# The head loop of a fused two-block transformer kernel: scores issued two heads ahead, and a projection tile moved in front of the loop

## The reference, cut to what matters

```
oa = moba_attention(qa, ka, heads(va, N_HEADS_A))
ob = dsa_attention(qb, kb, heads(vb, N_HEADS_B), qi, ki, wi)
oc = stick_breaking_attention(heads(qc, N_HEADS_C), ...)
...
log_1m = jnp.where(strict, jax.nn.log_sigmoid(-z), 0.0)
after = lax.cumsum(log_1m, axis=3, reverse=True) - log_1m
a = jnp.where(strict, jnp.exp(log_beta + after), 0.0)
...
o = (_rms(o).reshape(B, S, D_MIX) * out_g[layer]).astype(x.dtype)
x = x + g2 * (o @ w_out[layer])
```

## Time and profile before

| | |
|---|---|
| median of 3 runs | 2841.31 us (2838.57 to 2844.32) |
| the profiled execution | 2839.58 us |
| its span in the profile | 2837.5 us |
| granted TensorE clock, mean | 0.992 of 2.4 GHz |
| head loop, first layer | 2009.04 to 2060.49 us |
| head loop, second layer | 2564.74 to 2618.29 us |

### The profile page before, as it was taken

How to read it: one execution, slowest core, us unless ns; L and a number is a source line. 1 busy time by engine, 2 the same in 40 slices (tenths; PEclk the granted TensorE clock), 3 DMA queues, 4 the chain that set the end, 5 groups by cost and what they waited for, 6 DMA issues and landing times.

```text
span 2837.5 us, 37822 instructions
## 1 busy us (share of the span) xinstructions
PE 2766.8 (98%) x16120; PEld 2426.8 (86%) x16120; DVE 1951.3 (69%) x2187; ACT 1366.8 (48%) x1562; POOL 228.7 (8%) x201
## 2 busy tenths in 40 slices
PE   8999999999999999999999999999899999999999
PEld 6889999998888889999998887878878878788787
DVE  6668876655666678877655667677876676677644
ACT  5444545455444445545454444444644444446433
POOL 0000420000000000520000000003000000030000
PEclk9999999999999999999999999999999999998999
DMA  8655433445766655333446666653266676442454
GB/s 306 257 220 183 149 125 136 164 164 210 263 261 248 248 208 189 138 136 132 171 165 228 257 255 243 260 218 134 90 244 251 239 274 253 177 150 95 176 189 148
DMA packets 82038, 564.42 MB, mean 199 GB/s; under 512 B 9072, under 2 KB 10576, under 8 KB 15952
## 3 DMA queue, kind: packets, MB, share of 16 engines
q1 hardware_dynamic: 66272, 465.47, 44.8%
q0 software_dynamic: 15600, 96.55, 9.0%
HBM read 560.86 MB, written 1.12 MB: 198 GB/s over the span
## 4 chain that ended last, share of the span: by engine, by line
PE 78%; DVE 13%; ACT 4%; POOL 2%; issue 2%; DMA 1%; SPq 0%; POOLq 0%; ACTq 0%; DVEq 0%
PE ps L332 71%; DVE ring_lo L327 4%; ACT w_hi L320 2%; POOL qk L2038 1%; PE ps L899 1%; POOL rope_a L2034 1%; DVE a_hg L1806 1%; DMA rows<-mod_rows 1%; DMA ring<-stream 1%; DVE e L1786 1%; DVE e L1785 1%; PE ps L1287 1%; DVE h_lo L576 0%; PE ps L1416 0%; PE ps L1442 0%
## 5 line engine op out<-in xcount | busy, mean ns | idle before, releaser
L327 DVE TENSOR_TENSOR ring_lo<-ring,w_hi 128x2048 fp32r<-128x2048 f32 x422 | 973.8, 2310 | 484.0 <-ACT w_hi L320 473.0
L320 ACT ACTIVATE w_hi<-ring 128x2048 fp32r<-128x2048 f32 x422 | 806.4, 1911 | 318.6 <-PE ps L332 188.0
L332 PE MATMUL ps<-w_hi,h_hi 128*128 128x512 f32 (+1 forms) x1920 | 728.9, 380 | 18.1 <-DVE ring_lo L327 9.0
L332 PE MATMUL ps<-w_hi,h_lo 128*128 128x512 f32 (+1 forms) x1920 | 717.0, 373 | 0.0
L332 PE MATMUL ps<-ring_lo,h_hi 128*128 128x512 f32 (+1 forms) x1920 | 716.3, 373 | 0.0
L332 PEld LDWEIGHTS ps<-w_hi,h_hi 128*128 128x128 f32 x1920 | 363.7, 189 | 85.6 <-DVE ring_lo L327 11.3
L332 PE MATMUL ps<-h_hi,w_hi 128*128 128x256 f32 x1488 | 431.6, 290 | 1.4 <-DVE h_lo L576 1.3
L332 PE MATMUL ps<-h_lo,w_hi 128*128 128x256 f32 x1488 | 423.0, 284 | 0.0
L332 PE MATMUL ps<-h_hi,ring_lo 128*128 128x256 f32 x1488 | 423.0, 284 | 0.0
L332 PEld LDWEIGHTS ps<-w_hi,h_lo 128*128 128x128 f32 x1920 | 363.2, 189 | 64.7
L332 PEld LDWEIGHTS ps<-ring_lo,h_hi 128*128 128x128 f32 x1920 | 363.8, 189 | 60.7 <-issue 1.0
(11 more groups left out here) (359 smaller groups left out, 3437.4 us busy)
## 6 DMA issues: line engine op xcount, KB each, us to landing
ring<-stream SPq DMA_DIRECT2D x438, 1024.0 KB, 4.8
e<-ada POOLq DMA_DIRECT2D x77, 1024.0 KB, 6.2
rows<-mod_rows POOLq DMA_DIRECT2D x18, 512.0 KB, 5.7
rows<-gain_rows POOLq DMA_DIRECT2D x8, 512.0 KB, 4.8
val<-c_row POOLq DMA_DIRECT2D x4, 512.0 KB, 5.3
x<-x_in SPq DMA_DIRECT2D x4, 256.0 KB, 6.7
mem<-mem_t SPq DMA_DIRECT2D x1, 1024.0 KB, 16.2
out_t<-x SPq DMA_DIRECT2D x4, 256.0 KB, 2.1
```

The costliest lines, as they stand in the source:

```text
L320: nc.scalar.activation(hi_of(p), ring[:, p % RING, :], ACT.Copy).then_inc(S.w_hi_ready, 1)
L327: nc.vector.tensor_tensor(lo_of(p), ring[:, p % RING, :], hi_of(p).bitcast(F32), ALU.subtract).then_inc(S.w_lo_ready, 1)
L332: mm = nc.tensor.matmul(out, a, b, start=start and n == 0, stop=stop and n == 2, skip_group_check=group)
```

## The change

The same operations run in another order on three queues.

- TensorE: tile 13 is projected ahead of the loop, behind tile 12. Scores 0 and 1 come before the loop, then tile 14, and each step i issues scores i + 2 between the flip and the sums of head i - 1 (scores 4 at the end of step 2, since they need tile 14 copied out). `turn_back` stands between the two weighings. Tile 14 was in step 2. A wait for the last scores having been read goes. `out_part` only moves up in the text; its calls stay behind the loop.
- ScalarE: tiles 13 and 14 are copied out at the end of steps 0 and 1 instead of 1 and 3, and every step has one order. The high part for the output's last tile is made before the scaled copy of the last pair.
- VectorE: the stick logarithm of head i - 1 comes before the argument of head i - 2. The remainders of the first three output tiles come in steps 0, 1 and 2 instead of 1, 3 and 5, that of the last one before the last `pair_low`.

```
--- before.py
+++ after.py
-            for n in range(9, 13):
+            for n in range(9, 14):
                 tile(n)
...
-            scores_sticks(0)
-            for i in range(HEADS_2 + 2):
-                if i + 1 < HEADS_2:
-                    scores_sticks(i + 1)
-                if i in (0, 2):
-                    tile(13 + i // 2)
-                if 0 <= i - 1 < HEADS_2:
-                    flip(i - 1)
-                    sums(i - 1)
-                if i >= 5 and i % 2 == 1:
-                    turn_back((i - 5) // 2)
-                n = i - 2
-                if 0 <= n < HEADS_2:
-                    weigh(n, 0, n, pt2[:, n % 2, :], S.pt_ready, S.pv_done)
-                    weigh(n, 1, stick_head(n), st[:, 6 + n % 2, :], S.a_ready, S.o_done)
-            pe.wait_ge(S.arg_ready, nth(S.arg_ready, HEADS_2))
-            pe.wait_ge(S.scores_read, nth(S.scores_read, HEADS_2))
...
+            scores_sticks(0)
+            scores_sticks(1)
+            for i in range(HEADS_2 + 2):
+                n = i - 2
+                if i == 0:
+                    tile(14)
+                if 0 <= i - 1 < HEADS_2:
+                    flip(i - 1)
+                if i + 2 < HEADS_2 and i != 2:
+                    scores_sticks(i + 2)
+                if 0 <= i - 1 < HEADS_2:
+                    sums(i - 1)
+                if 0 <= n < HEADS_2:
+                    weigh(n, 0, n, pt2[:, n % 2, :], S.pt_ready, S.pv_done)
+                if i >= 5 and i % 2 == 1:
+                    turn_back((i - 5) // 2)
+                if 0 <= n < HEADS_2:
+                    weigh(n, 1, stick_head(n), st[:, 6 + n % 2, :], S.a_ready, S.o_done)
+                if i == 2:
+                    scores_sticks(4)
+            pe.wait_ge(S.arg_ready, nth(S.arg_ready, HEADS_2))
...
             for i in range(HEADS_2 + 4):
-                if 0 <= i - 2 < HEADS_2 and i != 3:
+                if 0 <= i - 2 < HEADS_2:
                     flipped(i - 2)
                 if i >= 5 and i % 2 == 1:
                     pair_rstd((i - 5) // 2)
                 if i < HEADS_2:
                     exps(i)
-                if i == 3:
-                    softplus(i)
-                    evac(14)
-                    flipped(i - 2)
                 if 0 <= i - 2 < HEADS_2:
                     sticked(i - 2)
+                if i == HEADS_2 + 3:
+                    next_high(act, Z_O)
                 if i >= 4 and i % 2 == 0:
                     pair_sq((i - 4) // 2)
                 if i >= 5 and i % 2 == 1:
                     pair_high((i - 5) // 2)
-                if i < HEADS_2 and i != 3:
+                if i < HEADS_2:
                     softplus(i)
-                if i == 1:
-                    evac(13)
-            next_high(act, Z_O)
+                if i < 2:
+                    evac(13 + i)
...
-                if i == 3:
-                    low(dve, Z_V + 6 + HIGHS)
+                if 0 <= i - 1 < HEADS_2:
+                    stick_log(i - 1)
+                if 0 <= i - 2 < HEADS_2:
+                    stick_arg(i - 2)
+                if i < 3:
+                    low(dve, Z_V + 5 + i + HIGHS)
                 if i >= 5 and i % 2 == 1:
                     pair_scaled((i - 5) // 2)
-                if 0 <= i - 2 < HEADS_2:
-                    stick_arg(i - 2)
-                if 0 <= i - 1 < HEADS_2:
-                    stick_log(i - 1)
-                if i == 1:
-                    low(dve, Z_V + 5 + HIGHS)
-                if i == 5:
-                    low(dve, Z_V + 7 + HIGHS)
                 if i >= 4 and i % 2 == 0:
                     pair_stat((i - 4) // 2)
+                if i == HEADS_2 + 3:
+                    low(dve, Z_O + HIGHS)
                 if i >= 5 and i % 2 == 1:
                     pair_low((i - 5) // 2)
...
-            low(dve, Z_O + HIGHS)
             shift_dve(dve, chain, 2, Z_O + 2, row_count + 6, 0, z_ready)
```

## The result

The changed kernel takes 2853.67 us (median of 5 runs, 2850.46 to 2855.89) against 2841.26 us (5 runs, 2835.76 to 2844.32): ratio 1.0047, interval 1.0032 to 1.0061, slower by 12.4 us. Forecast were 2849.7 us in a range of 2842.5 to 2857.

What follows compares the result with a forecast made beforehand. The prediction took a chain between three in-order queues in the second block's head loop as the bound. Start 3.2 plus steady part 1.0 us per layer, 8.4 in all, on 2841.3 gave 2849.7 us, range 2842.5 to 2857.

Steps and rivals of the forecast that it cites:

- What bounds it: Second block's head loop: a chain between three in-order queues, no engine full; gain or loss reaches the end one for one.
- The start: Loop start to scores 4: TensorE waits about 3.7 us for tile 13's copy before tile 14; cost 3.2 us per layer.
- The 3.2 us: Loop start: scores 4 start at 2031.3 instead of 2028.12, a cost of 3.2 us per layer.
- The steady part: From scores 4 to the projection: shorter waits before the sums are given back; 32.0 against 31.0 us, net 1.0 per layer.
- the delay of turn-back 0: Behind flip 4: scores 7 and a weighing now precede turn-back 0, making it 0.8 us later and delaying flip 5.
- The sum: Both layers: start 3.2 plus steady part 1.0 is 4.2 us per layer, 8.4 us slower in all.
- The clock, the mis-sized term: Both loops and projections: the kernel before loses 6.6 us to the lower clock; the main forecast added no further clock loss.
- the band of 2845 to 2854: Whole kernel time if the forecast holds as worked out; chance 0.52.
- the clock gets worse: Rival: tile 14 cold, 1.8 us per layer, and first layer losing 4.0 more; 2857 us, chance 0.18 for 2854 to 2860.
- Scores ahead pay: Rival, steady part: logarithm and flip waits vanish, 6.8 us per layer, 7.2 gained in all; 2834 us, chance 0.07.

Runs made afterwards that it cites:

- e1: Changed kernel with ScalarE copying tile 13 out before the exponentials and softplus of head 0, not behind them; 2844.12 us, ratio 1.0009.
- e5: Changed kernel with unread matmuls in TensorE's waits before tile 14, flip 6, sums 6, flip 7 and turn-back 2, none before flip 5; 2846.32 us, ratio 1.0025.
- e10: Kernel before with only the changed start, and unread matmuls in TensorE's waits before tile 14 and in the late waits; 2839.80 us, ratio 0.9997.
- e4: Kernel before with only the stick logarithm of head i - 1 ahead of the argument of head i - 2 on VectorE; 2843.29 us, ratio 1.0012.
- e8: Kernel before with only the scores issued two heads ahead; 2845.47 us, ratio 1.0016.
- e9: Kernel before with only the turn-back of a pair moved behind the first weighing of its step; 2847.96 us, ratio 1.0026.
- e2: Changed kernel with the start of the kernel before, keeping scores two ahead, logarithm first and turn-back between the weighings; 2846.58 us, ratio 1.0025.
- e6: Kernel before with unread matmuls in its late waits, before sums 5, sums 6, flip 7 and turn-back 2; 2833.10 us, ratio 0.9979.
- e7: Same operations as both kernels in a new order on all three queues, one VectorE remainder moved behind the loop; 2816.80 us, ratio 0.9915.
- e3: Kernel before with only the changed start: tile 13 ahead of the loop, tile 14 in step 0, copies and remainders earlier; 2856.81 us, ratio 1.0061.
- e11: Changed kernel with tile 13 copied out first and unread matmuls in the late waits before flip 6, sums 6, flip 7 and turn-back 2; 2840.46 us, ratio 1.0004.

## Why the prediction was right, and where a size was off

- *What bounds it.* Right. Three queues, no full engine, and the end follows one for one: the 12.9 us of the four stretches match the 12.4 us between the medians.
- *The start.* The events came as worked out: first score, first softening, a wait of 3.83 us (forecast 3.7) for line 2442, tile 14 at the forecast place within 0.2 us, and e1 shows that this wait carries most of the loss. Scores 4 came 1.7 us later than forecast, of which 1.4 is the cold tile 14. The 3.2 us, the delay of scores 4, are borne out at full clock: 3.6 in e5, 3.2 in e10 (22.99 us after the copy, against 19.82 before). The forecast did not say that ScalarE would be idle ahead of the copy, which is why the loss was so easy to undo. (Where it counts four weighings between flip 1 and scores 4, there are two; the 2.2 us are read from the row and hold.)
- *The steady part.* The reason holds: the waits changed names. The logarithm's wait became the argument's (e4), and flips 5 and 7 now wait 2.40 us for ScalarE's copy. Both parts of the delay of turn-back 0 count: in e8, with scores 7 ahead of it, flip 5 waits 1.73 us, in e9, with the weighing ahead, 1.54, before 0.87. Its size depends on the start. Behind the new start the old steady order makes up 1.0 us, so that e10 ends only 2.2 late; that leaves 1.9 for the steady part. Behind the old start it carries 3.2 (e2). So 3.2 + 1.0 is a split along the time of this one order, and only its sum, 4.2, can be priced by itself; I was wrong to use the terms as the costs of the two halves in e2.
- *The sum.* 8.4 us of queue order. No run has the whole changed order at full clock, so the 55.0 us are carried: e5 bears them out to within 0.4 us as far as flip 5, and the rest, 16.6 us, is not shown. For whole loops the method was within 0.3 us in e6, e7 and e10.
- *The clock, the mis-sized term.* The sum assumed that the clock would take the same 6.6 us as before. It took 6.6 in before (e6) and about 11.7 in the changed kernel: 5.7 and 5.4 us over the carried loops, 0.6 in the first projection. The 5 us between them are what the forecast was short of, and they brought 2853.67 us to the very edge of the band of 2845 to 2854 that I held most likely. It is the rival "the clock gets worse" in part: tile 14 went cold in both layers (1.4 and 2.7 us, forecast 1.8 each), while the second layer's projection, cold before, kept its clock. The Trainium skill, "TensorE: Matmul & The Clock Gate", HAM oscillation, says that a burst of matmuls behind a long wait starts cold; the trace agrees, 7.28 and 8.53 us for tile 14 against 5.85 and, with the wait filled, 5.94. My remark that the clock fell only in the loop's sparse stretches holds for the loops alone: elsewhere in the trace of before it fell too, to a mean of 0.52 from 2470 to 2480 us.
- *Scores ahead pay.* Refuted by e8 alone and by e2.

Open: why the halves e2 and e3 lose to the clock so unevenly between the two layers of one execution. Also open are the last 16.6 us of the changed loop at full clock and what it costs e8 beyond its queues. Filling the wait before flip 5 wasn't tried. The earlier remainder and high part of the output's last tile were only run together with the rest.

## What to carry to other kernels

In a stage where several in-order queues hand work to each other, ask of every operation that is issued earlier what now stands in front of the copy that frees its buffer: here one bank and one copy behind a softplus made most of the loss, while the engine that had to make the copy had been idle just before. Carry the queues through with the row durations before and after the change; where the clock held it was good to 0.3 us for a whole loop. Price the clock by itself, with unread matmuls in the waits, but see that none of them runs at the lower clock, where it outlasts its wait (e5, e11). The clock's share was 5 us beside 8 of queue order in the changed kernel, and in e7, whose order leaves no long wait, it was nothing.

## What the runs showed of the hardware that I had not expected

- The granted clock fell to 0.5 behind waits of 2.1 us (before, line 2327) and 2.4 us (changed kernel and e5, before flip 5), shorter than the new wait before tile 14. With unread matmuls in the late waits of the old steady order it stayed at 1.00 in both layers (e6, e10), and so it did in e7, whose order has no TensorE wait over 0.8 us.
- The clock multiplies small losses: a turn-back moved by one weighing (e9) is 1.2 us per layer in the queues and took loops from 52.2 and 54.3 to 56.9 us.
- Unread matmuls alone made the kernel before faster by 6.5 us, ratio 0.9979 (0.9970 to 0.9988). Once the clock is down such matmuls cost time: three of them, in place ahead of sums 6, take 0.83 us at full clock in e10 and 1.45 us at 0.5 in e5.
